# A row of cumulative decays for every partition: turned on TensorE per head, or written to memory once a layer and read back by a DMA

## The reference, cut to what matters

```python
beta = jax.nn.sigmoid(b)
g = -jnp.exp(a_log) * jax.nn.softplus(a + dt_bias)      # (token, head)
gc = jnp.cumsum(g, axis=-1)                             # within a chunk
diff = gc[..., :, None] - gc[..., None, :]
decay_strict = jnp.exp(jnp.where(strict, diff, -jnp.inf))
m = einsum('bhnid,bhnjd->bhnij', kb, k) * decay_strict
attn = einsum('bhnid,bhnjd->bhnij', q, k) * decay_incl
qd = q * jnp.exp(gc)[..., None]
```

## Time and profile before

| | |
|---|---|
| median of 3 runs | 2732.13 us (2731.01 to 2733.20) |
| the profiled execution's own time | 2732.36 us |
| its span, first to last instruction | 2730.6 us |
| granted TensorE clock, mean | 0.998 |
| PE busy | 2706.4 us, 99% |
| DVE / ACT / POOL busy | 58% / 40% / 10% |
| stages of the heads | about 410 to 810 us and 1770 to 2160 us of the span |

### The profile page before, as it was taken

One profiled execution on the slowest core, in us unless ns is written; L12 is line 12 of the kernel. 1 busy time (PEld: TensorE's weight loads), 2 busy tenths in 40 slices (PEclk: granted clock), 3 DMA queues, 4 the chain that ended last, 5 costly groups with the idle time before them and its releaser, 6 DMA issues.

```text
span 2730.6 us, 35870 instructions
## 1 busy us (share of the span) xinstructions
PE 2706.4 (99%) x13089; PEld 2258.0 (83%) x13089; DVE 1585.0 (58%) x2519; ACT 1096.1 (40%) x1842; POOL 262.1 (10%) x233
## 2 busy tenths in 40 slices
PE   8999999999999999999999999999999999999999
PEld 7888878888888888888888888787888888888887
DVE  5554357888885345553354543688888944455532
ACT  4222346666663232222322222565666623322221
POOL 0000022112220010000000000211211200100000
PEclk9999999999999999999999999999999999999999
DMA  5333337666654333333333333667767453333331
GB/s 155 100 92 106 98 86 150 113 141 130 126 126 101 95 89 104 93 100 93 102 93 100 92 97 87 118 125 118 134 127 138 108 108 93 92 100 94 94 100 65
DMA packets 478060, 292.53 MB, mean 107 GB/s; under 512 B 12060, under 2 KB 462756, under 8 KB 477956
## 3 DMA queue, kind: packets, MB, share of 16 engines
q1 hardware_dynamic: 462820, 236.57, 34.3%
q0 software_dynamic: 14976, 54.53, 10.5%
q10 hardware_dynamic: 160, 0.07, 0.0%
HBM read 234.51 MB, written 2.10 MB: 87 GB/s over the span
## 4 chain that ended last, share of the span: by engine, by line
PE 94%; DVE 3%; DMA 2%; ACT 1%; issue 0%; SPq 0%; POOL 0%; POOLq 0%; ACTq 0%; DVEq 0%
PE bank L455 92%; DMA w_lo<-raw 1%; PE bank L609 1%; PE bank L661 1%; DVE w_lo L1202 0%; DVE c_lo L1688 0%; ACT c_hi L1158 0%; DMA xin<-in_x 0%; PE bank L623 0%; DVE qa L1375 0%; DVE g_lo L1218 0%; PE bank L697 0%; ACT w_lo L845 0%; DVE sqb L1684 0%; DVE hf L1684 0%
## 5 line engine op out<-in xcount | busy, mean ns | idle before, releaser
L1202 DVE TENSOR_TENSOR w_lo<-raw,w_hi 128x1024 fp32r<-128x1024 f32 x343 | 424.0, 1237 | 547.0 <-ACT w_hi L839 546.8
L839 ACT ACTIVATE w_hi<-raw 128x1024 fp32r<-128x1024 f32 x447 | 471.4, 1056 | 671.3 <-PE bank L455 642.2
L455 PE MATMUL bank<-h_hi,w_hi 128*128 128x512 f32 x1504 | 587.1, 390 | 3.2 <-ACT va L973 2.1
L455 PE MATMUL bank<-h_hi,w_lo 128*128 128x512 f32 x1504 | 585.5, 389 | 0.0
L455 PE MATMUL bank<-h_lo,w_hi 128*128 128x512 f32 x1504 | 585.2, 389 | 0.0
L455 PE MATMUL bank<-g_hi,w_hi 128*128 128x512 f32 x928 | 383.1, 413 | 6.2 <-DMA w_lo<-raw 6.2
L455 PE MATMUL bank<-g_hi,w_lo 128*128 128x512 f32 x928 | 378.3, 408 | 0.0
L455 PE MATMUL bank<-g_lo,w_hi 128*128 128x512 f32 x928 | 369.8, 399 | 0.0
L455 PEld LDWEIGHTS bank<-h_hi,w_hi 128*128 128x128 f32 x1504 | 282.4, 188 | 62.9 <-issue 4.2
L455 PEld LDWEIGHTS bank<-h_hi,w_lo 128*128 128x128 f32 x1504 | 282.4, 188 | 59.0
L455 PEld LDWEIGHTS bank<-h_lo,w_hi 128*128 128x128 f32 x1504 | 282.4, 188 | 58.1
(11 more groups left out here) (260 smaller groups left out, 3367.2 us busy)
## 6 DMA issues: line engine op xcount, KB each, us to landing
raw<-in_w_in SPq DMA_DIRECT2D x128, 512.0 KB, 8.7
w_lo<-raw POOLq DMA_DIRECT2D x104, 512.0 KB, 7.3
raw<-in_ffn_w_gate SPq DMA_DIRECT2D x88, 512.0 KB, 3.8
raw<-in_ffn_w_up SPq DMA_DIRECT2D x88, 512.0 KB, 3.8
raw<-in_ffn_w_down SPq DMA_DIRECT2D x64, 512.0 KB, 4.0
raw<-in_ffn_w_down SPq DMA_DIRECT2D x32, 384.0 KB, 3.4
raw<-in_w_a_out SPq DMA_DIRECT2D x16, 512.0 KB, 4.0
raw<-in_w_b_out SPq DMA_DIRECT2D x16, 512.0 KB, 4.2
```

Source lines behind the costliest of these rows:

```text
L455: return nc.tensor.matmul(o, a, b, start=start, stop=stop, **kw)
L839: nc.scalar.activation(w_hi[c % SLOTS][:, :], raw[c % SLOTS][:, :], ACT.Copy).then_inc(hi_done, 1)
L1202: tt(w_lo[c % SLOTS][:, :], raw[c % SLOTS][:, :], w_hi[c % SLOTS][:, :].bitcast(F32), ALU.subtract).then_inc(lo_v, 1)
```

## The change

The row is no longer made by PE for every head. In the first head of each layer PE still makes it with four transpositions (`gr`), and one further transposition turns the 128 x 32 tile of all heads' cumulative sums into 32 rows of 128 (bank 5). ACT copies these to the tile `S`, POOL writes them to a buffer in memory by a DMA of 16 KB and waits until it has landed. For each of the seven later heads POOL issues one DMA that reads the head's four rows (2 KB) to all 128 partitions of `dec` (256 KB), one head ahead: in the loop of head rn, behind the w_lo DMA of tile c0+4 and a wait for PE's `y3`. ACT's `eg` moves to the front of its head's chain, ahead of `ksq`; for later heads it waits for that DMA and reads `dec` instead of bank 0. DVE's `dmin` waits for `eg` instead of `gr` and works in place on `dec`. POOL's wait for `gr` becomes one for `kT`.

```diff
-PE_STEPS = [x for x in PE_ORDER if x not in ("H", "so", "fb")]
+PE_STEPS = [x for x in PE_ORDER if x not in ("H", "gr", "so", "fb")]
-ACT_STEPS = ["thk", "thq", "XTI", "thv", "ksq", "eg", "decT", "kd", "n0", "n1"]
+ACT_STEPS = ["thk", "thq", "XTI", "thv", "eg", "ksq", "decT", "kd", "n0", "n1"]
+        gc_rows = nc.dram_tensor("gc_rows", (DEPTH, HEADS * NC, P), F32, kind="Internal").ap()
...
                         for c in range(NC):
                             m = nc.tensor.transpose(bank[0][:, c * P:c * P + P], whole(hs[:, HS_GC, c:c + 1]), ident)
-                        m.then_inc(*pe_dn.step(name))
+                        m.then_inc(gr_done, 1)
+                        nc.tensor.transpose(bank[5][0:HEADS * NC, 0:P], abw[:, 4, :, :].rearrange("p h c -> p (h c)"), ident).then_inc(gct_pe, 1)
...
                 def run_stage(name, rn):
+                    if name == "gr" and rn != l * 8:
+                        return
...
+                    if rn == l * 8:
+                        act.wait_ge(gr_done, l + 1)
+                        nc.scalar.activation(qd[:, :], bank[0][:, :], ACT.Exp).then_inc(*ac_dn.step("eg"))
+                    else:
+                        act.wait_ge(row_in, (rn - l) * 16)
+                        nc.scalar.activation(qd[:, :], dec[:, :], ACT.Exp).then_inc(*ac_dn.step("eg"))
                     pe_("kt")
...
                     ve("dmin")
-                    nc.scalar.activation(qd[:, :], bank[0][:, :], ACT.Exp).then_inc(*ac_dn.step("eg"))
                     nc.scalar.activation(dec[:, :], dec[:, :], ACT.Exp).then_inc(*ac_dn.step("decT"))
...
+                    if rn == l * 8:
+                        act.wait_ge(gct_pe, l + 1)
+                        nc.scalar.activation(S[0:HEADS * NC, :], bank[5][0:HEADS * NC, 0:P], ACT.Copy).then_inc(gct_a, 1)
...
                     nc.vector.tensor_copy(hsc[:, :, HS_GC, :], sums[:, 0])
+                    nc.vector.tensor_copy(abw[:, 4, :, :], sums[:, 0])
...
-                        pe_("gr")
+                        ac("eg")
+                        me("hs")
                         for c in range(NC):
-                            a = stt(out=dec[:, c * P:c * P + P], in0=bank[0][:, c * P:c * P + P], scalar=hs[:, HS_GC, c:c + 1], in1=cst[:, I_CAP, :],
+                            a = stt(out=dec[:, c * P:c * P + P], in0=(bank[0] if rn == l * 8 else dec)[:, c * P:c * P + P], scalar=hs[:, HS_GC, c:c + 1], in1=cst[:, I_CAP, :],
                                     op0=ALU.subtract, op1=ALU.min)
...
                                 if c == 0:
+                                    if rn == l * 8:
+                                        dve.wait_ge(gct_out, (l + 1) * 16)
                                     ts(S[:, :], bank[2][:, 0:P], 1.0, None, ALU.mult).then_inc(*ve_dn.step("s0"))
...
                         if before:
-                            pool.wait_ge(pe_dn.sem, pe_dn.after(rn, "gr"))
+                            ve("kT")
                             square_sum(rn - 1)
...
                         lo(Rd, G, c0 + t + 4)
+                        if t == 0 and rn is not None and rn != l * 8 + 7:
+                            if rn == l * 8:
+                                pool.wait_ge(gct_a, l + 1)
+                                pool.dma_start(out=gc_rows[l], in_=S[0:HEADS * NC, :]).then_inc(gct_out, 16)
+                                pool.wait_ge(gct_out, (l + 1) * 16)
+                            pool.wait_ge(pe_dn.sem, pe_dn.after(rn, "y3"))
+                            h = rn + 1 - l * 8
+                            row = gc_rows[l, h * NC:h * NC + NC, :].rearrange("(o c) i -> o (c i)", o=1)
+                            pool.dma_start(out=dec[:, :], in_=row.broadcast_to([P, SEQ])).then_inc(row_in, 16)
```

More of the change, by code:

```diff
@@ L256, in trunk @@
         ghi_done = sem("ghi_done")
+        gr_done = sem("gr_done")
+        gct_pe = sem("gct_pe")
+        gct_a = sem("gct_a")
+        gct_out = sem("gct_out")
+        row_in = sem("row_in")
         mrinv_done = sem("mrinv_done")
```

## The result

The changed kernel takes 2742.59 us (median of five runs, 2740.9 to 2745.2) against 2731.01 us (five runs, 2729.8 to 2733.2): ratio 1.0040, 95% interval 1.0027 to 1.0053. It is slower by 11.6 us where 2726.4 was forecast, and lies outside the range.

What follows compares the result with a forecast made beforehand. The prediction took PE, busy 99% of the span, to bound the kernel. From 2732.4 us it took 6.2 for the removed transpositions and added 0.2 for the extra one, all else 0: 2726.4 us, range 2723.5 to 2733.5.

Steps and rivals of the forecast that it cites:

- the part on eg and dmin: ACT and DVE, later heads: eg moved to the front, dmin starting unchanged at 467.3 to 467.4, NT gaining 0 to 0.2 us.
- POOL's part: POOL in 14 heads: square_sum starts 0.7 us sooner, row issue takes 0.86 us on an engine busy 10%; cost 0.
- PE's term: PE, 14 later heads: four transpositions gone, 0.44 us each head, 6.2 us off the path.
- rival C: PE transpositions: listed durations count in full, 14.7 us, 2717.7 us; or both w_lo waits vanish, 2720.2; chance 0.07.
- x2t's margin: PE at x2t: weight load late by 0.2 us at most, cost 0; upper bound 0.1 a head, 1.4 us.
- The traffic: POOL's DMA queue: 14 rows of 256 KB ahead of tile c0+5's w_lo; taken as 0, bounds -6.2 to 9.3 us.
- Rival B: POOL's queue: rows stuck in slow stretches delay the next w_lo by 4.7 us each; 2735.7 to 2745 us; chance 0.14.
- the extra transposition: PE, once a layer: one more transposition, 0.11 us each, 0.2 us added; bounds 0 and 0.8.
- Rival A: PE gives back 1 to 4 us, up to 1.4 at x2t, up to 3 from late w_lo; 2729 us; chance 0.24.

Runs made afterwards that it cites:

- e1: Changed kernel with POOL's square_sum waiting for dmin instead of kT, so the sum runs behind dmin; 2737.71 us, ratio 1.0018.
- e5: Changed kernel with POOL's square_sum cut to one column of 512, all else in place; 2728.76 us, ratio 0.9989.
- e4: Changed kernel with ACT copying the row from dec to bank 0, dmin and eg reading bank 0, eg in its old place; 2728.52 us, ratio 0.9980.
- e6: Kernel before the change with only POOL's square_sum wait moved from gr to kT; 2733.42 us, ratio 1.0001.
- e2: Kernel before the change with gr left out in the 14 later heads, nothing in its place, no rows; 2726.55 us, ratio 0.9980.
- e7: e4 with the row's DMA issued one w_lo later, behind that of tile c0+5; 2726.03 us, ratio 0.9977.
- e3: Changed kernel with gr kept in every head and bank 0 read as before; rows still travel, unused, dmin waiting for them; 2733.29 us, ratio 1.0003.
- e8: e4 with the row's DMA issued by ACT on its own hardware queue instead of by POOL; 2731.64 us, ratio 0.9997.

## Why the prediction was wrong

**The step that failed** is the part on eg and dmin: "with eg in gr's place it starts at the same time, 467.3 to 467.4", and, from there on, NT, which "gains between 0 and 0.2". dmin's start was right within 0.1 us. But the working took dmin's duration, 1.12 us, over from a row in which its operand was bank 0, and the diff put the operand elsewhere. What the runs showed in its place: with dec as the operand, and POOL's sum running, 2.13 us. e1 and e5 show that the operand alone is harmless (347 ns an operation); e4 and e6 show that the sum alone is. It takes both.

**POOL's part** had the other half: its square_sum "now ... starts with osq's end, 0.7 us sooner, which nobody waits for last". True of semaphores. I asked who waits for the sum, and not what runs beside it. Before, the sum (467.44 to 468.71) ran beside dmin, which read a bank.

The Trainium skill states this (SBUF — State Buffer, "Who interferes with whom"): a VectorE instruction with two inputs in on-chip memory contends with a GpSimd instruction that reads it; the section calls the contention an exclusive lock, in which the order of issue decides who blocks. The traces agree, with 0.34 us becoming up to 1.35, and 1.27 becoming 1.56. The same section counts `tensor_scalar` among those that can take the shared ports in a 2-port mode. skE, 0.15 becoming 0.80 in e1, is a `tensor_scalar` with a single on-chip input; that it was held is measured, that it ran in such a mode no run here shows. I had looked for a rule that speaks against the change among the DMA pages only.

**PE's term, 6.2 us: right.** e2 measured 2732.73 - 2726.55 = 6.2 us (3.0 to 7.9 by its interval), and head distances fell by 0.43 in e2 and e7. Start-to-start distances gave the value; the listed 272 ns would have given 14.7 (rival C), which lies outside e2's interval.

**x2t's margin: right.** The forecast let a load be up to 0.2 us late for nothing; in e2, e4 and e7 PE waits for x2T only in the first heads. But x2T came 0.7 to 0.9 us later than forecast: counted from kt's start in gr's place (466.75, now 669.00), 471.9 to 472.1 is 674.15 to 674.35, and it ended at 674.30 + 0.73 = 675.03. That is past the margin, and PE lost 0.9 us per head.

**The traffic, taken at 0: not told from 0.** e3 has a ratio of 1.0003 (-1.6 to +3.3 us). Against e2, which has no rows, the ratios of e4, e5 and e7 differ by 0, +2.5 and -0.8 us, each less than the 3.5 us or so that their two intervals make together. Rival B's mechanism, more waiting for w_lo, is in none of the profiles: in total 2.2 to 6.2 us in all of them, 6.2 in the kernel before. Its mark does come up in e3 and e1, a w_lo landing in 21.1 and 20.5 us right behind a row, with waits of 6.2 and 5.5 us; but the same w_lo took 20.1 us and cost 5.2 with no row ahead of it, and 20.4 and 5.4 in e6, which has no rows. So that lateness is not the rows'. The time ended inside rival B's range, 2735.7 to 2745, but not by its mechanism.

**The account.** Compare the two profiled executions first: spans of 2730.6 and 2739.1 us, 8.5 more. The undisturbed heads give 14 x 0.48 = 6.8 of it: 6.2 less for PE's term and 12.9 more for the collision. The heads with late transfers give 1.8 more: the two heads from 491.26 to 594.44 have the 2.2 us wait for kT, behind a wait of ACT of 6.3 us for a raw fetch, while in the second layer PE waits less for w_lo. The rest of the span gives -0.1; the 0.2 us of the extra transposition are not seen in it. The profiled execution of the changed kernel, 2740.9 us, is its quickest and 1.7 us under its median, and that of before is 1.4 us over the 2731.0; these 3 us of the 11.6 lie in executions without a profile and stay open, and so does whether the kT wait has to do with the change (e6, without rows, has 0.3 us of it in the same head, e2 and e7 none).

**Rival A** named waits for x2T in 14 places as its mark, and that is what came, but it priced them at 0.1 us a head, taking x2T's lateness to be only what PE had gained. It was 0.9, from an instruction that had become longer: the right mark for another reason.

## What to carry to other kernels

When an operand moves from PSUM to on-chip memory, its instruction's duration is no longer that of the old row: here a VectorE instruction with a second on-chip input and a GpSimd instruction that reads on-chip memory held each other up, in both directions. So list for every moved operand what GpSimd runs in that window, by start and end times, not by semaphores. A copy to PSUM by an idle ScalarE (0.60 us each, 14 of them, hidden: heads of 48.60 us as in e2) was the cheap way out and turned 11.6 us lost into 4 to 7 won (e4, ratio 0.9980, and e7, 0.9977); moving the GpSimd instruction only moved the collision to the next VectorE step.

## What the runs showed of the hardware that was not expected

- The exclusion is one of whole instructions and goes both ways within two microseconds: the tap holds the sum (1.27 to 1.56 us), the sum holds dmin (0.34 to 1.34 us).
- Size is no protection: an operation of 128 x 4 elements was held for 0.65 us.
- A 512-column VectorE operation with one input in PSUM and one on-chip (og, 0.73 us) runs beside GpSimd's sum without loss, and so does the sum (1.28 us in e1).
- A row of 2 KB read to 128 partitions lands in 5.3 us on GpSimd's queue between w_lo transfers, and in 3.6 us on ScalarE's; one w_lo later on GpSimd's queue (e7) it takes 8.6 us. The time did not follow the landing: e7, with the slowest rows, has the lowest median, and in none of e4, e7 and e8 does ACT's copy wait for a row.
